# Prompt attention of a decoder trunk: who takes the outputs out of PSUM and splits them

## The reference

```
s = einsum('bqhd,bkhd->bhqk', q, k) / sqrt(64) + (cq - ck)     # forgetting attention
p = softmax(where(mask, s, -inf))
o = einsum('bhqk,bkhd->bqhd', p, v)
h = h + o @ w_o
h = h + square(relu(rmsnorm(h, g) @ w_up)) @ w_down
```

## Time and profile before

| what | value |
|---|---|
| median of 3 runs | 2588.94 us (2585.78 to 2590.66) |
| profiled execution | 2592.62 us, span 2590.5 us |
| TensorE matmul busy | 2405.4 us (93% of the span) |
| VectorE busy | 1083.8 us (42%) |
| ScalarE busy | 594.1 us (23%) |
| GpSimd busy | 607.2 us (23%) |
| mean granted TensorE clock | 0.944 of full speed |

### The profile page before, as it was taken

One profiled execution on the slowest core, in us unless ns is written; L12 is line 12 of the kernel. 1 busy time (PEld: TensorE's weight loads), 2 busy tenths in 40 slices (PEclk: granted clock), 3 DMA queues, 4 the chain that ended last, 5 costly groups with the idle time before them and its releaser, 6 DMA issues. The chain is left out here.

```text
span 2590.5 us, 36154 instructions
## 1 busy us (share of the span) xinstructions
PE 2405.4 (93%) x14092; PEld 2193.4 (85%) x14092; DVE 1083.8 (42%) x1794; ACT 594.1 (23%) x1276; POOL 607.2 (23%) x398
## 2 busy tenths in 40 slices
PE   3289999999999999999788899999999999999998
PEld 2289999999999967777566666669999999999997
DVE  5864333324333666430101377763443343333331
ACT  3242001101101433331111366652211011011001
POOL 1062322323323512000100011125432332332321
PEclk6599999999999999999666799999999999999999
DMA  3011111111111225331522244421111111111111
GB/s 114 3 33 50 47 44 50 42 49 49 42 49 41 82 85 171 106 117 45 146 82 82 61 111 115 111 54 41 49 41 49 49 42 50 49 41 50 41 50 76
DMA packets 191776, 169.05 MB, mean 65 GB/s; under 512 B 28304, under 2 KB 168640, under 8 KB 191623
## 3 DMA queue, kind: packets, MB, share of 16 engines
q1 hardware_dynamic: 150681, 136.92, 18.5%
q10 hardware_dynamic: 40950, 30.02, 3.6%
HBM read 136.77 MB, written 30.50 MB: 65 GB/s over the span
## 5 line engine op out<-in xcount | busy, mean ns | idle before, releaser
L310 PE MATMUL ps<-xn_hi,w_lo 128*128 128x352 f32 x1584 | 515.8, 326 | 63.1 <-DVE h L1667 39.0
L310 PE MATMUL ps<-xn_lo,w_hi 128*128 128x352 f32 x1584 | 510.5, 322 | 0.0
L310 PE MATMUL ps<-xn_hi,w_hi 128*128 128x352 f32 x1584 | 510.0, 322 | 0.0
L539 PE MATMUL ps<-hid_hi,w_lo 128*128 128x352 f32 x1536 | 495.4, 323 | 0.0
L539 PE MATMUL ps<-hid_lo,w_hi 128*128 128x352 f32 x1536 | 492.7, 321 | 0.0
L539 PE MATMUL ps<-hid_hi,w_hi 128*128 128x352 f32 x1536 | 492.2, 320 | 0.0
L288 POOL CAST w_hi<-w_raw 128x1024 fp32r<-128x1024 f32 x138 | 144.8, 1050 | 1134.7 <-issue 530.0
L609 DVE TENSOR_TENSOR h<-ps,h 128x352 f32<-128x352 f32 x384 | 198.5, 522 | 446.3 <-PE ps L539 446.3
L310 PEld LDWEIGHTS ps<-xn_hi,w_lo 128*128 128x128 f32 x1584 | 299.4, 189 | 66.8 <-DVE xn_lo L1661 39.3
L577 ACT ACTIVATE tmp_b<-tmp_a 128x352 f32<-128x352 f32 x192 | 95.3, 499 | 1091.1 <-DVE tmp_a L595 1091.1
L290 POOL TENSOR_TENSOR w_lo<-w_raw,w_hi 128x1024 fp32r<-128x1024 f32 x138 | 332.9, 2412 | 11.0
(11 more groups left out here) (191 smaller groups left out, 2738.1 us busy)
## 6 DMA issues: line engine op xcount, KB each, us to landing
w_raw<-in_w_up SPq DMA_DIRECT2D x64, 512.0 KB, 4.1
w_raw<-in_w_down SPq DMA_DIRECT2D x64, 512.0 KB, 3.4
out<-tok_out ACTq DMA_DIRECT2D x32, 256.0 KB, 2.1
qk_dram<-turn_hi ACTq DMA_DIRECT2D x32, 256.0 KB, 2.4
qk_dram<-turn_lo ACTq DMA_DIRECT2D x32, 256.0 KB, 2.9
k_pg<-in_cache_k SPq DMA_DIRECT2D x16, 512.0 KB, 3.7
v_pg<-in_cache_v SPq DMA_DIRECT2D x16, 512.0 KB, 4.2
q_a<-qk_dram SPq DMA_DIRECT2D x32, 256.0 KB
```

Source lines behind the costliest of these rows:

```text
L310: last = pe.matmul(ps[:, bank, 0:CH], w, x(k, c), start=(k == 0 and i == 0), stop=(k == nk - 1 and i == 2))
L539: last = pe.matmul(ps[:, NC * (dm % 2) + c, 0:CH], w, x, start=(k == 0 and i == 0), stop=(k == GT - 1 and i == 2))
```

## The change

ScalarE gets a new step `high` that copies both halves of an output group from PSUM straight into `o_hi`. It stands in step 5 of a head (first group of this head) and in step 3 (second group of the head before), each time behind `turned` and `exp`, and once after the loop. VectorE's `out` keeps its places, but waits for ScalarE's half and writes `o_lo` as the PSUM tile minus `o_hi`, in place of the copy to `oT`. GpSimd's splits of the eight pairs are gone; it splits the sample columns and then at once the two weight blocks of `w_o`. The projection waits for VectorE's count in place of GpSimd's. `oT` holds the sample columns only.

```diff
@@ ProjO.pe
-                            before = lambda k: pe.wait_ge(o_cut, 2 + 2 * (k + 1))
+                            def before(k):
+                                pe.wait_ge(o_cut, 2)
+                                pe.wait_ge(o_ev, 8 * (k + 1))
@@ prompt_act
+            def high(n):
+                hh, g = n // NQ, n // 4 % 2
+                e, av = hh % 2, 2 * hh + g
+                for q in range(2):
+                    act.wait_ge(o_full, 2 * av + q + 1)
+                    c = 512 * g + 256 * q
+                    act.activation(o_hi[HD * e:HD * e + HD, hh // 2, c:c + 256],
+                                   ps[HD * q:HD * q + HD, 6 + av % 2, 0:256], ACT.Copy).then_inc(o_high, 1)
+
             for n in range(3):
                 exp(n)
             for n in range(NBLK):
                 turned(n)
                 if n + 3 < NBLK:
                     exp(n + 3)
+                if n % NQ == 5:
+                    high(n - 2)
+                elif n % NQ == 3 and n > NQ:
+                    high(n - 4)
+            high(NBLK - 1)
@@ prompt_dve, out
-                    dve.wait_ge(o_full, 2 * av + q + 1)
+                    dve.wait_ge(o_high, 2 * av + q + 1)
                     c = 512 * g + 256 * q
-                    dve.tensor_copy(oT[HD * e:HD * e + HD, hh // 2, c:c + 256],
-                                    ps[HD * q:HD * q + HD, 6 + av % 2, 0:256]).then_inc(o_ev, 1)
+                    o = slice(HD * e, HD * e + HD)
+                    dve.tensor_tensor(o_lo[o, hh // 2, c:c + 256], ps[HD * q:HD * q + HD, 6 + av % 2, 0:256],
+                                      o_hi[o, hh // 2, c:c + 256].bitcast(F32), ALU.subtract).then_inc(o_ev, 1)
@@ prompt_pool
-            def cut_o_pair(r):
-                pool.wait_ge(o_ev, 8 * (r + 1))
-                cut_o(r + 1, r, slice(0, T))
-
             cut_o(0, slice(0, KT), slice(T, N))
-            for r in range(NP - 1):
-                cut_o_pair(r)
             split_one(pool, n_of["o"])
             split_one(pool, n_of["o"] + 1)
-            cut_o_pair(NP - 1)
```

More of the change, by code:

```diff
@@ L1003, in decoder_step @@
              "afull", "aev", "const", "cc"))
-        (c_done, c_sent, one_rows, cut, q_full, q_max, q_exp, q_rec, q_nrm, t_full, t_ev, o_full, o_ev, a_const) = (
+        (c_done, c_sent, one_rows, o_high, q_full, q_max, q_exp, q_rec, q_nrm, t_full, t_ev, o_full, o_ev, a_const) = (
             sem("pa_" + n) for n in
-            ("c", "csent", "ones", "cut", "full", "max", "exp", "rec", "nrm", "tr", "tev", "ofull", "oev", "const"))
+            ("c", "csent", "ones", "ohigh", "full", "max", "exp", "rec", "nrm", "tr", "tev", "ofull", "oev", "const"))
         stacked = [sem("pa_stk0"), sem("pa_stk1")]
```

## The result

| | before | changed |
|---|---|---|
| median of 7 runs each | 2590.66 us | 2603.03 us |
| range | 2585.78 to 2595.64 | 2601.92 to 2606.96 |
| span of the profiled execution | 2590.5 us | 2599.8 us |

The change makes the kernel slower by 0.50% (ratio 1.0050, 95% interval 1.0038 to 1.0062), 12.4 us between the medians. Forecast were 2598.1 us and slower with a chance of 0.62; the time lies inside the range of 2585 to 2606, but above the forecast's own one of 2594 to 2602 and nearer to the 2604 of rival C.

A forecast was written before the change was run, and what follows sets the result against it. TensorE was taken to bound most of a head, but a ScalarE-VectorE chain the change of heads. Terms: -10.3 - 0.7 + 2.0 + 18.2 = +9.2 us, so 2598.1 against a median of 2588.94; range 2585 to 2606.

The forecast's parts named there:

- rival C: Pair or semaphore hops dearer, 1.5 us per head, and head 0 longer at low clock: +15, 2604 us; chance 0.14.
- GpSimd's contention: Prompt attention: without GpSimd's split, whose subtraction holds VectorE's scaling, seven long heads get shorter: -10.3 us.
- The last split: Ahead of the output projection: TensorE no longer waits for GpSimd before the eighth k: -0.7 us.
- (b): Block 5 of a head: ScalarE's pair and VectorE's wait delay the next head's block 1 maximum: 0.40 us more per head.
- The moved splits: Head 0, first blocks: GpSimd's two w_o splits now run there and hold VectorE's scalings: +2.0 us.
- The added wait and copies: Change of heads: ScalarE's copies and VectorE's wait for them, (a) and (b) over 15 heads each: +18.2 us.
- (a): Block 3 of a head: VectorE waits for ScalarE's pair, so block 7's maximum comes 0.81 us late, in 15 heads.
- A: Faster: ScalarE's copies hide in its idle time, cost below 0.60 us per head: -9.0, 2579.9 us; chance 0.14.
- B: Half hidden: (a) costs, (b) does not: +3.2, 2592.1 us; chance 0.20.
- D: GpSimd's contention is not the cause of the long heads, nothing gained there: +19.5, 2608.4 us; chance 0.02.

The follow-up runs named there:

- e2_cast_only: Kernel before, with GpSimd's subtraction for the eight pairs of heads replaced by a second cast, leaving out the low part: 2579.51 us, ratio 0.9958.
- e1_early_split: Changed kernel, with GpSimd's two w_o weight splits ahead of its wait for the sample attention: 2599.98 us, ratio 1.0042.
- e8_out_after_top: As e1_early_split, with VectorE's subtractions behind the row maximum in steps 4 and 6, ScalarE's pairs untouched: 2585.00 us, ratio 0.9974.
- e3_no_wait: Changed kernel without VectorE's wait for ScalarE, both reading another tile, so the attention outputs are not split: 2586.14 us, ratio 0.9989.
- e4_b_moved: Changed kernel, with the first group's ScalarE pair moved to step 1 of the next head and its subtractions to step 2: 2596.16 us, ratio 1.0019.
- e5_slack: Changed kernel with e1_early_split and e4_b_moved together, and VectorE's subtractions behind the row maximum of their step: 2579.25 us, ratio 0.9949.
- e9_halves: As e5_slack, with the second group's halves taken apart: ScalarE in steps 2 and 3, VectorE in steps 3 and 4: 2577.56 us, ratio 0.9945.
- e7_before_early: Kernel before, with GpSimd's two w_o splits ahead of its wait for the sample attention: 2591.23 us, ratio 0.9996.
- e6_slack_before_top: As e5_slack, but with VectorE's subtractions ahead of the row maximum of their step: 2593.15 us, ratio 1.0005.

## Why the prediction was right, and where its sizes were off

**GpSimd's contention, forecast -10.3.** Undisturbed heads take 16.57 us (e2_cast_only), so the kernel before held 258.17 - 15 x 16.57 = 9.6 us of it. The forecast took 16.48 from the first interval, which is the shortest of all. That the subtraction is the cause is shown by e2_cast_only. The scaling does not end with it, as the prediction reads the rows, but 0.49 us behind it (1508.98 against 1508.49); the sum does not use this.

**The last split, forecast -0.7.** TensorE has no wait ahead of the eighth k after the change; its first product starts 0.3 us later behind the last maximum than before (9.99 against 9.69), and the waits ahead of its last two turns are 1.22 and 0.74 us where they were 0.65 and 0.45. The prediction counted nothing for (b) in head 15. Right in kind and nearly in size.

**The moved splits, forecast +2.0, measured +3.2.** The first stretch takes 15.53 us where it took 12.36. The first turn of head 0 comes 4.76 us behind the first score (1455.67 to 1460.43), before it was 3.42: 1.3 us, close to the 1.5 forecast. The other part is TensorE's clock. Products of 512 columns that take 0.48 us at full speed take 0.78 in head 0. Before, the last slow one starts at 1466.51, 6.9 us behind the first score; after the change this row still shows it 13.8 us behind:

```profile
1469.49 0.78 PE L1238 MATMUL ps<-k_a,q_a 128*128 128x512 f32 x1
```

The prediction had this mechanism in rival C and not in the sum. It is the term that was under-sized: the first stall was priced, what it does to the clock was not. e1_early_split shows that it goes with the splits.

**The added wait and copies, forecast +18.2.** In e1_early_split, where no clock drop disturbs them, the heads sum to 266.09, that is 266.09 - 248.55 = 17.5 us above undisturbed ones, 1.17 per head against 1.21. The first steps are the forecast ones. From the scaling of block 5 to the maximum of block 7 it is 2.23 us in one kind of head (1523.55 to 1525.78) and 2.37 in the other (1541.30 to 1543.67), against 1.43 before (1555.95 to 1557.38): late by 0.80 and 0.94, forecast 0.81. From there to the turn of block 6 it is 3.1 us before and after, so the whole delay gets to TensorE.

Three readings behind that were not right. TensorE's wait ahead of the turn of block 6 is 0.98 us and not 1.2, since 0.18 to 0.32 us of the delay now comes ahead of the turn of block 5: ScalarE's pair stands ahead of the pT copies of block 4, which the prediction took to cost nothing. The heads are not alike, but alternate between 17.6 and 17.9. And (b) is not only the late maximum of block 1. In e8_out_after_top the subtractions are behind it and wait for nobody, and the place of the first group's work still costs 0.48 us per head, with TensorE waiting for the pT copies of block 6; in e3_no_wait, without the wait, 0 or 0.5 is left in a head. So (b) was right in size, but ScalarE's own time carries a part of it that the prediction gave to VectorE's late maximum, and how the two share it in the changed kernel is open. No experiment prices (a) and (b) by themselves either. e4_b_moved, with the pair of step 4 alone, lies 17.30 - 16.57 = 0.73 above an undisturbed head, forecast 0.81, and 0.44 below e1_early_split, forecast 0.40.

One number was wrong without harm to the sum. Two copies on ScalarE were to overlap by 0.1 us and to take 0.66; they take 0.77 to 0.78. The lost overlap that the prediction left out of its sum shows where it was expected: behind the subtractions of an odd head the reciprocal starts 1.26 us after the maximum (1543.67 to 1544.93), behind those of an even one 1.14 (1525.78 to 1526.92). But the exponential starts 1.26 us behind the maximum in both, so it costs nothing there.

**What no term had: +2.9.** In two of the fifteen intervals the clock falls, and each is 1.4 us longer than its like (19.31 against 17.89). With it the sum is -9.6 + 17.5 + 2.9 = +10.8, the measured difference of the interval sums, 268.94 - 258.17; with +3.2 for the first stretch, +0.3 and -0.7 it gives +13.5 (the terms are rounded one by one, the sum is not). So the forecast of +9.2 is short by 2.9 of clock drops, 1.2 in head 0, and 0.3 at the end. Its two large terms were each 0.7 too large, with opposite signs, and cancel: that is luck.

**The rivals.** A fails at its own condition: the cost is 1.17 us per head where it needed less than 0.60. What spoke for it, idle time of 1 us ahead of each long exponential, is real; e5_slack and e9_halves use this idle time and reach A's time (2577.6 to 2579.3, A had 2579.9), with two helps that A did not count on: the early splits, and the output instructions behind the maximum. The copies could have been hidden there, but the changed kernel puts them, and above all VectorE's wait, at the change of heads, where there is no slack. B is out: both parts cost. Of C, the clock part was right (it had +3.5 for head 0) and the dearer pair was not (1.17 per head where it had 1.5); that the time lies near its 2604 comes in part from the clock drops in two heads and from the higher starting point, neither of which it had. D is out by e2_cast_only.

## What to carry to other kernels

An engine's mean share of busy time says nothing about where a new wait may stand: ask, at the place itself, whether the instruction behind it starts with no idle time, and whether another engine stands waiting for what it leads to. Where both held here, a maximum late by 0.80 to 0.94 us made the head 0.73 longer (e4_b_moved), whatever slack the engine had elsewhere, and an exchange of two calls was worth 0.88 us in each of 15 heads. Ask the same of the engine that does the added work: its pair of copies delayed what was queued behind it. And work that is freed of a wait moves to another place, where it must be priced again, as the two weight splits show.

## What the runs showed of the hardware

**Clock drops in a busy stage.** TensorE's mean granted clock is 0.91 of full speed in the two long heads, and its products take 0.67 us where they take 0.42, the durations that it has in head 0 at the lower of its levels, 1.2 GHz. From 1494.1 to 1497.4 us the granted clock is 0.53. In both profiles of the changed kernel the drops begin with the turn of block 7, behind waits of 0.98 and 0.79 us:

```profile
1491.93 0.95 PE L1253 MATMUL ps<-ident,p_lo 128*128 128x128 f32 x7 [0.98 <-ACT pT L1307]
...
1493.98 1.64 PE L1253 MATMUL ps<-ident,p_hi 128*128 128x128 f32 x8 [0.79 <-ACT pT L1307]
1495.27 0.67 PE L1238 MATMUL ps<-k_a,q_a 128*128 128x384 f32 x1
```

e7_before_early has one such head, behind a wait of 1.47 us, and e6_slack_before_top one behind waits of 1.22 and 0.74 us in the last head, where the table does not count it: its first product of the projection comes 12.9 us behind the last maximum, against 10.0 in the changed kernel. But most heads with the same waits keep the full clock, and the profile of e1_early_split, whose waits are the same to 0.01 us, has no drop at all:

```profile
1490.75 0.96 PE L1253 MATMUL ps<-ident,p_lo 128*128 128x128 f32 x7 [0.98 <-ACT pT L1307]
...
1492.80 1.06 PE L1253 MATMUL ps<-ident,p_hi 128*128 128x128 f32 x8 [0.79 <-ACT pT L1307]
```

What picks the heads stays open; that the same two were picked in two profiles speaks against chance. Nor is it known how often e1_early_split drops outside its one profile: its median is only 3.1 us below the changed kernel's, while the first stretch alone is 3.5 us shorter. None of the profiles of e2, e3, e4, e5, e8 and e9 has a head of this kind, though e4_b_moved has the waits of 0.98 us.

**ScalarE's pairs do not overlap when they change partitions.** The two halves, on partitions 0 to 63 and 64 to 127 of PSUM, take 0.77 to 0.78 us, as 0.38 each one after the other, where two pT copies overlap by 0.1 us. In e3_no_wait, where the input of both halves starts on the same partition of a tile in SBUF, a half takes 0.41 and the pair 0.72, so they do overlap by 0.1; the memory is another one there too, so that this is a hint and no proof. Behind the accumulator read the pair starts 0.10 us after the read's start in heads whose output lies on partitions 0 to 63 (1524.38 to 1524.48), and 0.21 after it in the others, as below; in step 5 it is 0.09 (1547.03 to 1547.12) and 0.25 (1529.13 to 1529.38).

```profile
1506.62 0.19 ACT L1296 ACTIVATION_READ_ACCUMULATOR p_lo<-ps,stat 128x1 f32 x1
1506.83 0.78 ACT L1316 ACTIVATE o_hi<-ps 64x256 fp32r<-64x256 f32 x2
```

The two differences, 0.11 and 0.16, would account for 0.27 of the 0.29 us by which heads of 17.6 and 17.9 us alternate. The Trainium skill (VectorE: DVE Perf Modes, Two Vector instructions with no wait between them) describes such holding by the start quadrant for VectorE; these rows show the like on ScalarE. It was not tested by an experiment of its own.
